# Later modulation rows computed by output columns: a multiply-and-sum along each row on VectorE in place of running sums and a sum over partitions on TensorE

## The chip, the cores and the metric

The kernel runs on one core of one Trainium2 chip. The metric is the device time of one execution in microseconds (us), lower is better. A core has TensorE (PE; its weight loads are listed apart as PEld), VectorE (DVE), ScalarE (ACT), GpSimd (POOL) and SyncE (SP); SP, ACT and POOL also issue DMA transfers.

## The reference, cut to what matters

One layer of a diffusion backbone, batch 1, 1024 tokens of 1024 channels, a context of 256 tokens, everything in float32:

```python
mod_x = jax.nn.silu(c) @ w_ada[l] + b_ada[l]                 # c: (1, 1024), w_ada: (1024, 6 * 1024)
sh1, sc1, g1, sh2, sc2, g2 = jnp.split(mod_x[:, None, :], 6, axis=-1)
h_x = _modulate(_rms_norm(x, norm1_gain[l]), sh1, sc1)       # h * (1 + scale) + shift
y_x, y_c = _token_mixer(h_x, h_c, ...)                       # Fourier branch, retention branch, gates, y @ w_out
x = x + g1 * y_x
h2 = _modulate(_rms_norm(x, norm2_gain[l]), sh2, sc2)
x = x + g2 * _sq_relu_mlp(h2, w_mlp1[l], w_mlp2[l])
return _rms_norm(x, final_gain)
```

Of the six modulation rows of 1024 values, the first two (sh1, sc1) are needed before any projection can start. The change concerns the other four: g1, sh2, sc2 and g2.

## The kernel before, in words

Nearly all the time is TensorE's. Each float32 product of the large projections is made of three products of operands split into a rounded part ("hi") and a remainder ("lo"): `mm3` and its relatives. Weights stream in chunks through a ring: SP loads a chunk into `raw` (256 or 512 KB transfers), ACT writes `ring_hi` (`hi_to`), and POOL subtracts (`lo`, line 1005) to make `ring_lo`. SP loads chunk i only when POOL is done with chunk i-2. All engines run programs written out by hand, each in its own order, joined by semaphores.

The stages in order: modulation rows sh1, sc1 and the input projections (0 to about 350 us); the Fourier and retention output products `four_product`, `ret_product` (to about 435); the gates with Strassen-like products `gate_product` (to about 590); the output projection `out_first`, `out_first_end`, `out_step` with the 16 chunks ("wo", 0) to ("wo", 15) (to about 680); the two MLP products (to the end).

**The output projection**, where most of the rows below lie: it makes 16 groups i of 128 tokens by 512 columns. Groups 0 to 3 are `out_first`; steps 1, 2 and 3 make groups 4 to 7, 8 to 11 and 12 to 15. In steps 1 and 2 the four groups advance together, chunk by chunk, so that all four end shortly one after the other, and group i+4 starts in the PSUM bank that group i has left. It may start when VectorE has done `residual` for that group (two operations, lines 2355 and 2357), which TensorE learns from `o_free`:

```python
if kp == 0:
    pe.wait_ge(o_free, i - 3)
```

**The later modulation rows.** `load_ada(eng, j)` loads, for j = 0 to 31, the 128 x 1024 block of `w_ada` of 128 input channels (j % 8) and of one of the four rows (j // 8), 512 KB each, from 128 rows of the matrix that lie 24 KB apart. `add_row(j)` on VectorE multiplies the block by the 128 values of silu(c) that stand one to a partition, and adds it to a running sum: in `ada_acc` in SBUF for j below 16; for the rest, but the last block of each row, in two banks of PSUM (`ps`). After eight blocks the sum over the 128 partitions is still missing: `reduce_row(a, bank)` on TensorE multiplies `ada_acc` by a column of ones, two halves of 512 columns, in plain float32. It is called four times: after two of the gate products, in step 1 after the last chunk of group 4, and in step 2 before the last chunk. `row_out(a, banks)` on ACT copies the two results out of PSUM (line 1311) and stores them in `mod_scr` in DRAM; g1 and g2 come back from there as broadcast tiles `g1b`, `g2b`, and sh2, sc2 as `mod2`, one value to a partition.

The order that matters on VectorE: in the output projection `residual(0, 0..3)`, then `add_row(18..26)`, then `residual(1, 0..3)`, then `add_row(27..29)`, `z_mean(0, 4)`, the sums on `mod2`, `add_row(30)`, `add_row(31)`. On ACT the loads of blocks 22 to 31 stand between the `hi_to` calls for chunks 7 to 12; each waits until the row that used its buffer before is done. Blocks 18 to 21 are loaded by SP before.

Of the kernel before, what the change touches and what calls it, by code (L numbers as in the profile page):

```python
# [21 lines left out]
P = 128  # L22
D = 1024
# [112 lines left out]
def program(nc, ins, out):  # L136
    with ExitStack() as ctx:
# [141 lines left out]
        hss = small("hss", [P, 3, NT, HEADS])  # L279
        cols = small("cols", [P, 2, 2])  # L280
# [38 lines left out]
        ada_acc = place("ada_acc", o_t + 2048, [P, D])  # L319
        ada_row = place("ada_row", o_t + 6144, [64, 512])  # L320
# [54 lines left out]
        mod_scr = nc.dram_tensor("mod_scr", [4, D], F32, kind="Internal").ap()  # L375
# [71 lines left out]
        ada_acc_done = sem("ada_acc_done")  # L447
        ada_red = sem("ada_red")
        ada_row_out = sem("ada_row_out")
        row_stored = sem("row_stored")  # L450
# [79 lines left out]
        def load_ada(eng, j):  # L530

            if j == 0:
                yr_stored(eng, 1)
            elif j < 18:
                eng.wait_ge(ada_acc_done, j)
            elif j < 21:
                gate_wait(eng, 5, KT - 1)
            else:
                eng.wait_ge(ada_acc_done, {29: 27, 30: 28, 31: 30}.get(j, j - 3))
# [188 lines left out]
        def _(sp):  # L728
# [229 lines left out]
            for s in range(2, STEPS):  # L958
# [5 lines left out]
                if s == 2 * FP + 1:  # L964
                    sp.wait_ge(row_stored, 16 * 8)
                    sp.dma_start(g2b[:], mod_scr[3:4, :].to_broadcast([P, D])).then_inc(gates_in, 16)
# [92 lines left out]
        def _(act):  # L1059
# [166 lines left out]
            for j in range(1, 18):  # L1226
# [77 lines left out]
            def row_out(a, banks):  # L1304

                for half in range(2):
                    act.wait_ge(ada_red, 2 * a + half + 1)
                    if a:
                        act.wait_ge(row_stored, 32 * a)
                    row = ada_row[32 * half:32 * half + 1, :]  # L1310
# [17 lines left out]
            def g_copy(p, m):  # L1328
# [7 lines left out]
                else:  # L1336
# [5 lines left out]
                    else:  # L1342
                        act.wait_ge(ada_acc_done, 4)
# [19 lines left out]
            hi_to(("fo", 2))  # L1363
            load_ada(act, 0)
# [49 lines left out]
            for j in range(1, KT - 3):  # L1414
# [6 lines left out]
                if j == 2:  # L1421
                    row_out(0, 2)
# [12 lines left out]
            row_out(1, 2)  # L1435
# [29 lines left out]
            act.dma_start(g1b[:], mod_scr[0:1, :].to_broadcast([P, D])).then_inc(gate1_in, 16)  # L1465
# [11 lines left out]
            row_out(2, 0)  # L1477
            hi_to(("wo", 10))
            load_ada(act, 29)
            act.wait_ge(row_stored, 16 * 6)  # L1480
            with nc.allow_non_contiguous_dma(reason="2048 modulation values, one per row"):
                for a in range(2):
                    act.dma_start(mod2[:, a, :], mod_scr[1 + a, :].rearrange("(c p) -> p c", p=P)).then_inc(gates_in, 16)
            hi_to(("wo", 11))

            def z_square(t):
                row_added(act, t)
                act.wait_ge(sumsq, 10 + t)
                if t in (0, 4):

                    act.wait_ge(ada_row_out, 6 + t // 2)
# [81 lines left out]
            row_out(3, 0)  # L1573
# [15 lines left out]
            act.wait_ge(row_stored, 16 * 8)  # L1589
# [187 lines left out]
        def _(dve):  # L1777
# [356 lines left out]
            def add_row(jj):  # L2134

                kt = jj % 8
                src = ada_place(jj)
                late = jj >= 16
# [3 lines left out]
                if kt == 7 and late or kt == 0 and 0 < jj < 16:  # L2142

                    dve.wait_ge(ada_red, 2 * (jj // 8))
                if jj == 16:
                    dve.wait_ge(ada_row_out, 4)
                if kt == 0:
                    do.chain(V.tensor_scalar(total, src[:], silu_c[:, 0, 0:1], None, ALU.mult), ada_acc_done)
                else:
                    do.chain(V.scalar_tensor_tensor(ada_acc[:] if kt == 7 else total, src[:], silu_c[:, kt, 0:1], total,  # L2150
                                                    ALU.mult, ALU.add), ada_acc_done)
# [315 lines left out]
            dve.wait_ge(gates_in, 16 * 2)  # L2467
# [20 lines left out]
            dve.wait_ge(row_stored, 16 * 8)  # L2488
# [186 lines left out]
            for s in range(3, STEPS):  # L2675
                down_los(s)
                q, n = s // FP, s % FP
                if s == 2 * FP + 4:
                    dve.wait_ge(gates_in, 16 * 5)
# [41 lines left out]
        def _(pe):  # L2721
# [293 lines left out]
            def reduce_row(a, bank):  # L3015

                pe.wait_ge(ada_acc_done, 8 * (a + 1))
                if a:
                    pe.wait_ge(ada_row_out, 2 * a)
                if a == 2:  # L3020
                    pe.wait_ge(o_free, 4)
                if a == 3:
                    pe.wait_ge(sumsq, 14)
                for half in range(2):
                    M(ps[32 * half:32 * half + 1, bank + half, :], lhsT=ones[:],
# [423 lines left out]
```

## Time and profile before

| | before |
|---|---|
| median of 3 runs | 1307.93 us (1307.86 to 1310.1) |
| profiled execution: from the first to the last instruction (span) | 1306.3 us; its time as a whole is not listed apart, the median lies 1.6 us above the span |
| busy: PE | 1278.7 us (98%) |
| busy: DVE | 875.5 us (67%) |
| busy: ACT | 605.1 us (46%) |
| busy: POOL | 147.0 us (11%) |
| chain that ended last | PE 93%, DVE 3%, DMA 2% |

Busy time is the union of an engine's instructions. A row of the timeline gives the start, the duration, the engine, the line of the kernel, the operation, what it writes and reads by the program's names, and in brackets how long the engine stood idle before it and what ended that. Neighbouring instructions of one kind are merged ("x3"). Matmuls overlap, so that their spacing, not their listed duration, is what one costs.

### The profile page before, as it was taken

To read this page: it belongs to the slowest core of one execution; us is meant where nothing else is said; L and a number is where in the kernel's file an instruction comes from. 1 tells how busy PE (TensorE), PEld (TensorE's weight loads), DVE (VectorE), ACT (ScalarE), POOL (GpSimd) and SP (SyncE) were. 2 spreads that over 40 slices of the span, in tenths; PEclk is the share of its full clock that TensorE was granted. 3 is DMA by queue.
4 is the path that set the end of the run, shared out by engine and by line. 5 is a ranking of instruction groups with operands and counts; after the bars stand their busy time and mean duration, and the time that the engine had idled before them with its cause. 6 is when DMAs were issued, how large, how long until landed. Compare 5 with 4: busy or idle time off the path is not lost.

```text
span 1306.3 us, 16741 instructions
## 1 busy us (share of the span) xinstructions
PE 1278.7 (98%) x6140; PEld 1044.1 (80%) x6140; DVE 875.5 (67%) x1397; ACT 605.1 (46%) x1039; POOL 147.0 (11%) x87
## 2 busy tenths in 40 slices
PE   5999999999999999999999999999999999999997
PEld 1788788888888778888788888888888888888886
DVE  3563577752556987768588766556646568868866
ACT  6871221242123544452668655545555433554444
POOL 0216330102231000014530000000000000000000
PEclk8999999999999999999999999999999999999999
DMA  9414220202256455567852544444438986468634
GB/s 382 154 33 146 81 97 1 65 13 66 65 191 219 146 193 202 182 252 278 297 185 73 191 155 161 137 149 162 151 114 281 316 281 222 162 215 266 192 100 162
DMA packets 95098, 220.09 MB, mean 168 GB/s; under 512 B 12436, under 2 KB 12692, under 8 KB 93992
## 3 DMA queue, kind: packets, MB, share of 16 engines
q1 hardware_dynamic: 83184, 189.58, 42.8%
q10 hardware_dynamic: 10040, 23.15, 4.9%
q0 software_dynamic: 1792, 6.29, 1.4%
q8 instruction: 49, 0.80, 0.3%
q14 instruction: 33, 0.27, 0.1%
HBM read 167.59 MB, written 51.40 MB: 168 GB/s over the span
## 4 chain that ended last, share of the span: by engine, by line
PE 93%; DVE 3%; DMA 2%; issue 1%; ACT 1%; POOL 0%; SPq 0%; ACTq 0%; DVEq 0%
PE ps L2726 16%; PE ps L2728 15%; PE ps L2727 15%; PE ps L3266 8%; PE ps L3274 8%; PE ps L3269 8%; PE ps L3109 4%; PE ps L3104 4%; PE ps L3106 4%; PE ps L3292 3%; PE ps L2804 2%; DMA ada_in<-in_w_ada 2%; PE ps L2930 1%; PE ps L2912 1%; PE ps L2871 1%
## 5 line engine op out<-in xcount | busy, mean ns | idle before, releaser
L1005 POOL TENSOR_TENSOR ring_lo<-raw,ring_hi 128x1024 fp32r<-128x1024 f32 x42 | 102.7, 2458 | 500.4 <-ACT ring_hi L1088 500.3
L2726 PE MATMUL ps<-t_hi,s_hi 128*128 128x512 f32 x392 | 153.1, 391 | 0.0
L2728 PE MATMUL ps<-t_hi,s_lo 128*128 128x512 f32 x392 | 153.1, 391 | 0.0
L2727 PE MATMUL ps<-t_lo,s_hi 128*128 128x512 f32 x392 | 153.1, 390 | 0.0
L1646 ACT ACTIVATE s_hi<-s_raw 128x512 fp32r<-128x512 f32 x112 | 70.5, 630 | 115.2 <-DMA b<-in_w_stream 58.1
L2605 DVE TENSOR_TENSOR s_lo<-s_raw,s_hi 128x512 fp32r<-128x512 f32 x112 | 77.3, 690 | 44.5 <-ACT s_hi L1646 44.0
L2726 PE MATMUL ps<-ring_hi,hT_hi 128*128 128x512 f32 x232 | 94.2, 406 | 0.0
L2728 PE MATMUL ps<-ring_hi,hT_lo 128*128 128x512 f32 x232 | 90.7, 391 | 0.0
L2727 PE MATMUL ps<-ring_lo,hT_hi 128*128 128x512 f32 x232 | 90.5, 390 | 0.0
L2726 PEld LDWEIGHTS ps<-t_hi,s_hi 128*128 128x128 f32 x392 | 73.6, 188 | 16.2 <-DVE t_lo L2609 0.4
L2727 PEld LDWEIGHTS ps<-t_lo,s_hi 128*128 128x128 f32 x392 | 73.6, 188 | 15.9
L2728 PEld LDWEIGHTS ps<-t_hi,s_lo 128*128 128x128 f32 x392 | 73.6, 188 | 15.8
L1088 ACT ACTIVATE ring_hi<-raw 128x1024 fp32r<-128x1024 f32 x46 | 48.2, 1057 | 70.7 <-DMA raw<-in_w_stream 35.3
L1634 ACT ACTIVATE ffa<-ffa 128x512 f32<-128x512 f32 x48 | 30.3, 631 | 71.2 <-DVE ffa L2543 71.2
L2543 DVE TENSOR_TENSOR ffa<-ps,uw 128x512 f32<-128x512 f32 x32 | 22.1, 691 | 44.9 <-PE ps L3274 25.0
L2726 PEld LDWEIGHTS ps<-ring_hi,hT_hi 128*128 128x128 f32 x232 | 43.6, 188 | 10.5 <-issue 1.5
L2728 PEld LDWEIGHTS ps<-ring_hi,hT_lo 128*128 128x128 f32 x232 | 43.5, 188 | 9.6
L3266 PE MATMUL ps<-h_hi,w_T_hi 128*128 128x512 f32 x128 | 50.1, 391 | 0.0
L2727 PEld LDWEIGHTS ps<-ring_lo,hT_hi 128*128 128x128 f32 x232 | 43.7, 188 | 8.0
L3266 PE MATMUL ps<-h_hi,w_B_hi 128*128 128x512 f32 x128 | 50.0, 391 | 0.0
L3269 PE MATMUL ps<-h_lo,w_T_hi 128*128 128x512 f32 x128 | 49.9, 390 | 0.0
L3269 PE MATMUL ps<-h_lo,w_B_hi 128*128 128x512 f32 x128 | 49.8, 389 | 0.0
(474 smaller groups left out, 3151.6 us busy)
## 6 DMA issues: line engine op xcount, KB each, us to landing
s_raw<-ff_scr SPq DMA_DIRECT2D x112, 256.0 KB, 2.9
raw<-in_w_stream SPq DMA_DIRECT2D x34, 512.0 KB, 4.3
ff_scr<-ffs SPq DMA_DIRECT2D x16, 1024.0 KB, 4.8
t_raw<-in_w_stream SPq DMA_DIRECT2D x64, 256.0 KB, 3.5
w_B_raw<-in_w_stream SPq DMA_DIRECT2D x48, 256.0 KB, 2.8
ff_scr<-ffa SPq DMA_DIRECT2D x16, 768.0 KB, 4.5
b<-in_w_stream SPq DMA_DIRECT2D x48, 256.0 KB, 4.3
ada_in<-in_w_ada SPq DMA_DIRECT2D x8, 1024.0 KB, 14.9
```

The costliest lines, as they stand in the source:

```text
L1005: nc.gpsimd.tensor_tensor(lo_ap, raw_of(i), hi_ap.bitcast(F32), ALU.subtract).then_inc(split, 1)
L1646: A(s_slot[n][0][:], s_slot[n][2][:], ACT.Copy).then_inc(down_hi, 1)
L2605: V.tensor_tensor(s_slot[n][1][:], s_slot[n][2][:], s_slot[n][0][:].bitcast(F32), ALU.subtract).then_inc(down_lo, 1)
L2726: M(dst, lhsT=l_hi, rhs=r_hi, start=first, stop=False, skip_group_check=goes_on)
L2727: M(dst, lhsT=l_hi, rhs=r_lo, start=False, stop=False, skip_group_check=goes_on)
L2728: return M(dst, lhsT=l_lo, rhs=r_hi, start=False, stop=last, skip_group_check=goes_on)
L3104: M(ps[:, b, :], lhsT=l_hi[:, w], rhs=m_hi[:, kt, :], start=kt == 0 and not adds, stop=False, skip_group_check=adds)
L3106: M(ps[:, b, :], lhsT=l_hi[:, w], rhs=m_lo[:, kt, :], start=False, stop=False, skip_group_check=adds)
L3109: mm = M(ps[:, b, :], lhsT=l_lo[:, kt * P:(kt + 1) * P], rhs=m_hi[:, kt, :], start=False, stop=kt == 3, skip_group_check=adds)
L3266: M(ps[:, b, :], lhsT=l_hi[:, w], rhs=m_hi[:, kt, :], start=kt == 0 and not adds, stop=False, skip_group_check=adds)
L3269: M(ps[:, b, :], lhsT=l_hi[:, w], rhs=m_lo[:, kt, :], start=False, stop=False, skip_group_check=adds)
L3274: mm = M(ps[:, b, :], lhsT=l_lo[:, w], rhs=m_hi[:, kt, :], start=False, stop=kt == 3 and (p, j) != (6, 0), skip_group_check=adds)
```

## The change

The host splits `w_ada`: the first 2048 columns stay as they are (`w_ada`, now with rows of 8 KB that follow one another), and the last 4096 columns are transposed into `ada_columns`, 32 blocks of 128 output columns by 1024 input channels, each 512 KB in one piece. silu(c) is laid out once along the free dimension: ACT stores `silu_c` to DRAM (`silu_scr`, 1024 values of 4 bytes) and, when the Fourier split is done (`ab_ready`, 7), loads it back as `silu_row`, 128 x 1024, the same row in every partition. `add_row(j)` is then one `tensor_tensor_reduce` on VectorE: block times `silu_row`, summed along the row, 128 finished modulation values, one to a partition. Blocks 8 to 23 write straight into `mod2`; blocks 0 to 7 and 24 to 31 (g1, g2) into `gate_cols`, which ACT stores (`store_gate`) for the broadcast loads. `reduce_row` and `row_out` are gone, with their waits. The loads have the same size, number and order, and the waits for their buffers are the same.

```diff
-        mod_scr = nc.dram_tensor("mod_scr", [4, D], F32, kind="Internal").ap()
+        gate_scr = nc.dram_tensor("gate_scr", [2, D], F32, kind="Internal").ap()
+        silu_scr = nc.dram_tensor("silu_scr", [1, D], F32, kind="Internal").ap()
...
-            eng.dma_start(ada_place(j)[:], ins["w_ada"][(j % 8) * P:(j % 8 + 1) * P, (2 + j // 8) * D:(3 + j // 8) * D]
-                          ).then_inc(ada_landed(j)[0], 16)
+            eng.dma_start(ada_place(j)[:], ins["ada_columns"][j]).then_inc(ada_landed(j)[0], 16)
...
                 if j == 12:
                     act.wait_ge(masked, NT)
+                    with nc.allow_non_contiguous_dma(reason="1024 values of c, one per row"):
+                        act.dma_start(silu_scr[0].rearrange("(c p) -> p c", p=P), silu_c[:, :, 0]).then_inc(silu_stored, 16)
...
-            def row_out(a, banks):
-
-                for half in range(2):
-                    act.wait_ge(ada_red, 2 * a + half + 1)
...
-                    A(row, ps[32 * half:32 * half + 1, banks + half, :], ACT.Copy).then_inc(ada_row_out, 1)
-                    act.wait_ge(ada_row_out, 2 * a + half + 1)
-                    act.dma_start(mod_scr[a:a + 1, half * 512:(half + 1) * 512], row).then_inc(row_stored, 16)
+            def store_gate(a):
+
+                act.wait_ge(mod_done, (8, 32)[a])
+                with nc.allow_non_contiguous_dma(reason="1024 modulation values, one per row"):
+                    act.dma_start(gate_scr[a].rearrange("(c p) -> p c", p=P), gate_cols[:, a, :]).then_inc(gate_stored, 16)
...
+            act.wait_ge(ab_ready, 7)
+            act.wait_ge(silu_stored, 16)
+            act.dma_start(silu_row[:], silu_scr[0:1, :].to_broadcast([P, D])).then_inc(silu_in, 16)
             load_ada(act, 0)
...
-            row_out(1, 2)
...
-            row_out(2, 0)
             hi_to(("wo", 10))
             load_ada(act, 29)
-            act.wait_ge(row_stored, 16 * 6)
-            with nc.allow_non_contiguous_dma(reason="2048 modulation values, one per row"):
-                for a in range(2):
-                    act.dma_start(mod2[:, a, :], mod_scr[1 + a, :].rearrange("(c p) -> p c", p=P)).then_inc(gates_in, 16)
             hi_to(("wo", 11))
...
             def add_row(jj):
 
-                kt = jj % 8
+                a, c = jj // 8, jj % 8
                 src = ada_place(jj)
...
-                total = ps[:, 2:4, :].rearrange("p a b -> p (a b)") if late else ada_acc[:]
+                total = gate_cols[:, a // 3, c:c + 1] if a in (0, 3) else mod2[:, a - 1, c:c + 1]
+                if jj == 0:
+                    dve.wait_ge(silu_in, 16)
                 dve.wait_ge(*ada_landed(jj))
...
-                    do.chain(V.scalar_tensor_tensor(ada_acc[:] if kt == 7 else total, src[:], silu_c[:, kt, 0:1], total,
-                                                    ALU.mult, ALU.add), ada_acc_done)
+                do.chain(V.tensor_tensor_reduce(src[:], src[:], silu_row[:], 1.0, 0.0, ALU.mult, ALU.add, total), mod_done)
...
-            dve.wait_ge(gates_in, 16 * 2)
             do.chain(V.tensor_tensor(mod2[:], mod2[:], bmod2[:], ALU.add))
...
-            def reduce_row(a, bank):
-
-                pe.wait_ge(ada_acc_done, 8 * (a + 1))
...
-                for half in range(2):
-                    M(ps[32 * half:32 * half + 1, bank + half, :], lhsT=ones[:],
-                      rhs=ada_acc[:, half * 512:(half + 1) * 512],
-                      start=True, stop=True).then_inc(ada_red, 1)
...
-                        if (step, kp, t) in ((1, 3, 0), (2, 2, 3)):
-                            reduce_row(step + 1, 0)
...
-        "w_ada": a["w_ada"][0], "b_ada": b_ada,
+        "w_ada": a["w_ada"][0][:, :2 * D], "b_ada": b_ada,
+        "ada_columns": a["w_ada"][0][:, 2 * D:].T.reshape(32, P, D),
```

How it moves instructions, at two places. First VectorE in the output projection, between the last `residual` of groups 0 to 3 and the first of groups 4 to 7. Before (`ada_late_...` and `ada_next` are the four buffers of the loaded blocks, `ps` is PSUM):

```order
L2357 TENSOR_TENSOR acc<-ps,acc 128x512
L2150 SCALAR_TENSOR_TENSOR ps<-ada_late_198,silu_c,ps 128x1024
L2150 SCALAR_TENSOR_TENSOR ps<-ada_late_199,silu_c,ps 128x1024
L2150 SCALAR_TENSOR_TENSOR ps<-ada_late_200,silu_c,ps 128x1024
L2150 SCALAR_TENSOR_TENSOR ps<-ada_next,silu_c,ps 128x1024
L2150 SCALAR_TENSOR_TENSOR ps<-ada_late_198,silu_c,ps 128x1024
L2150 SCALAR_TENSOR_TENSOR ada_acc<-ada_late_199,silu_c,ps 128x1024
L2148 TENSOR_SCALAR ps<-ada_late_200,silu_c 128x1024
L2150 SCALAR_TENSOR_TENSOR ps<-ada_next,silu_c,ps 128x1024
L2150 SCALAR_TENSOR_TENSOR ps<-ada_late_198,silu_c,ps 128x1024
L2355 TENSOR_TENSOR ps<-ps,g1b 128x512
```

The same place in the changed kernel, its last three rows and the first `residual` (`mod_139` is `mod2`; the second instruction of each pair writes the sum out):

```order
L2340 TENSOR_TENSOR acc<-ps,acc 128x512
L2134 ISA ada_late_198,mod_139<-ada_late_198,silu_row 128x1024
L2134 ISA mod_139 128x1
...
L2134 ISA ada_late_200,gate_cols<-ada_late_200,silu_row 128x1024
L2134 ISA gate_cols 128x1
L2134 ISA ada_next,gate_cols<-ada_next,silu_row 128x1024
L2134 ISA gate_cols 128x1
L2134 ISA ada_late_198,gate_cols<-ada_late_198,silu_row 128x1024
L2134 ISA gate_cols 128x1
L2338 TENSOR_TENSOR ps<-ps,g1b 128x512
```

The nine rows keep their place; each is now two instructions, and its second operand of full width lies in SBUF (`silu_row`) and no longer in PSUM.

Second ACT at the same time, from the load of block 26 to the rounding of chunk 11. Before (`ring_hi<-raw` is `hi_to`):

```order
L542 DMA ada_late_198<-in_w_ada 128x1024
L542 DMA ada_late_199<-in_w_ada 128x1024
L542 DMA ada_late_200<-in_w_ada 128x1024
L1311 ACTIVATE ada_row<-ps 1x512
L1313 DMA mod_scr<-ada_row 1x512
L1311 ACTIVATE ada_row<-ps 1x512
L1313 DMA mod_scr<-ada_row 1x512
L1088 ACTIVATE ring_hi<-raw 128x1024
L542 DMA ada_late_198<-in_w_ada 128x1024
L1483 DMA mod_139<-mod_scr 128x8x1 x2
L1088 ACTIVATE ring_hi<-raw 128x1024
```

The same place in the changed kernel:

```order
L543 DMA ada_late_198<-in_ada_columns 128x1024
L543 DMA ada_late_199<-in_ada_columns 128x1024
L543 DMA ada_late_200<-in_ada_columns 128x1024
L1088 ACTIVATE ring_hi<-raw 128x1024
L543 DMA ada_late_198<-in_ada_columns 128x1024
L1088 ACTIVATE ring_hi<-raw 128x1024
```

The copies out of PSUM, their stores and the two loads of `mod2` are gone, and the rounding of chunks 10 and 11 follows the loads directly.

## Rows read from the trace of the kernel before

**Rows 1.** Waits of PE over the span: total us, times, longest us

```profile
PE ps L2830 <- DMA ada_in<-in_w_ada: 15.1, 7, 9.0
...
PE ps L3109 <- DVE g_B_lo L2214: 0.6, 1, 0.6
```

**Rows 2.** Timeline of PE around the third reduce_row: start us, duration us, instruction

```profile
627.61 0.39 PE L2727 MATMUL ps<-ring_lo,yT_hi 128*128 128x512 f32 x1
627.84 0.39 PE L2728 MATMUL ps<-ring_hi,yT_lo 128*128 128x512 f32 x1
628.15 1.03 PE L3025 MATMUL ps<-ada_acc,ones 128*1 128x512 f32 x4
629.11 0.50 PE L2726 MATMUL ps<-ring_hi,yT_hi 128*128 128x512 f32 x1
629.45 0.39 PE L2727 MATMUL ps<-ring_lo,yT_hi 128*128 128x512 f32 x1
```

**Rows 3.** Groups of VectorE by shape, add_row with its sum in PSUM: busy us, mean ns

```profile
L2150 DVE SCALAR_TENSOR_TENSOR ps<-ada_late,silu_c,ps 128x1024 f32<-128x1024 f32 x9 | 11.6, 1290 | 0.4 <-DMA ada_late<-in_w_ada 0.2
```

**Rows 4.** Timeline of VectorE at 307 us, a tensor_tensor_reduce of 512 columns

```profile
307.80 0.69 DVE L2069 CUSTOM_DVE_ANT_0 fj<-u_e,sgn 128x512 f32<-128x512 f32 x1
308.41 0.08 DVE L2069 DVE_READ_ACCUMULATOR2_ANT u_c<- 128x1 f32 x1
```

**Rows 5.** Timeline of VectorE, 594 to 602 us

```profile
594.10 1.23 DVE L2344 TENSOR_TENSOR yT_lo<-yf_in,yT_hi 128x1024 fp32r<-128x1024 f32 x1
595.68 2.99 DVE L2237 TENSOR_TENSOR sig<-sig,yr_in 128x1024 f32<-128x1024 f32 x1 [0.35 <-ACT sig L1358]
598.70 3.30 DVE L2248 TENSOR_TENSOR yf_in<-yf_in,sig 128x1024 f32<-128x1024 f32 x1
```

**Rows 6.** Timeline of POOL at the same time

```profile
595.15 5.77 POOL L1005 TENSOR_TENSOR ring_lo<-raw,ring_hi 128x1024 fp32r<-128x1024 f32 x2 [18.63 <-ACT ring_hi L1088]
```

**Rows 7.** Timeline of POOL, 612 to 635 us

```profile
612.41 4.91 POOL L1005 TENSOR_TENSOR ring_lo<-raw,ring_hi 128x1024 fp32r<-128x1024 f32 x2 [2.27 <-ACT ring_hi L1088]
622.73 4.75 POOL L1005 TENSOR_TENSOR ring_lo<-raw,ring_hi 128x1024 fp32r<-128x1024 f32 x2 [5.40 <-ACT ring_hi L1088]
632.43 2.40 POOL L1005 TENSOR_TENSOR ring_lo<-raw,ring_hi 128x1024 fp32r<-128x1024 f32 x1 [4.95 <-ACT ring_hi L1088]
```

**Rows 8.** Timeline of VectorE, rows 18 to 26 and the residual behind them

```profile
612.44 3.94 DVE L2150 SCALAR_TENSOR_TENSOR ps<-ada_late,silu_c,ps 128x1024 f32<-128x1024 f32 x3
...
621.78 1.28 DVE L2150 SCALAR_TENSOR_TENSOR ada_acc<-ada_late,silu_c,ps 128x1024 f32<-128x1024 f32 x1 [2.62 <-DMA ada_late<-in_w_ada]
625.73 1.29 DVE L2148 TENSOR_SCALAR ps<-ada_late,silu_c 128x1024 f32<-128x1024 f32 x1 [2.67 <-DMA ada_late<-in_w_ada]
...
629.70 0.70 DVE L2355 TENSOR_TENSOR ps<-ps,g1b 128x512 f32<-128x512 f32 x1
```

**Rows 9.** Timeline of PE, the first matmul of group 8

```profile
633.33 0.39 PE L2726 MATMUL ps<-ring_hi,yT_hi 128*128 128x512 f32 x1
```

**Rows 10.** Timeline of ACT, the last z_norm before the transposes

```profile
649.08 1.13 ACT L1506 ACTIVATE xa<-acc,rstd 128x1024 f32<-128x1024 f32 x1
```

**Rows 11.** Timeline of PE, the first transposes that read it

```profile
652.19 1.04 PE L2804 MATMUL ps<-ident,xa 128*128 128x128 f32 x8
```

**Rows 12.** Timeline of VectorE, the operation after add_row(0)

```profile
382.42 0.69 DVE L2164 COPY b_sb<-ps 128x512 f32<-128x512 f32 x1 [0.48 <-PE ps L3060]
```

**Rows 13.** Timeline of ACT, hi_to(("fo", 2)), ahead of the first block's load

```profile
372.90 1.06 ACT L1088 ACTIVATE ring_hi<-raw 128x1024 fp32r<-128x1024 f32 x1 [0.49 <-ACT yr_first L1298]
```

**Rows 14.** Instructions on g1b, a broadcast load of 1024 values: us to landing

```profile
DMA to landing us min/median/max: 6.8/6.8/6.8
```

**Rows 15.** Timeline of POOL at the time of add_row(0)

```profile
378.98 2.41 POOL L1005 TENSOR_TENSOR ring_lo<-raw,ring_hi 128x1024 fp32r<-128x1024 f32 x1 [2.55 <-ACT ring_hi L1088]
```

**Rows 16.** Timeline of PE, four_product(4), which needs VectorE's work behind add_row(0)

```profile
385.74 0.48 PE L2726 MATMUL ps<-ab_hi,ring_hi 128*128 128x512 f32 x1
```

**Rows 17.** Windows of PE in the head: busy, granted clock, DMA share, GB/s

```profile
18.00:28.00 10.00, 6.47 (x28) 0.53 1.01 419
```

More of the change, by code:

```diff
@@ L279, in program @@
         hss = small("hss", [P, 3, NT, HEADS])
+        gate_cols = small("gate_cols", [P, 2, KT])
         cols = small("cols", [P, 2, 2])
@@ L318, in program @@
         b_sb = place("b_sb", o_t, [P, HALF])
-        ada_acc = place("ada_acc", o_t + 2048, [P, D])
-        ada_row = place("ada_row", o_t + 6144, [64, 512])
+        silu_row = place("silu_row", o_t + 2048, [P, D])
         yr_first = [place("yr_first0", o_kv + 12288, [P, SEQ]), place("yr_first1", o_t + 16384, [P, SEQ])]
@@ L446, in program @@
         ada_raw_in = sem("ada_raw_in")
[L447 to L450, printed above, removed]
+        mod_done = sem("mod_done")
+        silu_stored = sem("silu_stored")
+        silu_in = sem("silu_in")
+        gate_stored = sem("gate_stored")
         acc_in = [sem(f"acc_in{i}") for i in range(4)]
@@ L534, in load_ada @@
             elif j < 18:
-                eng.wait_ge(ada_acc_done, j)
+                eng.wait_ge(mod_done, j)
             elif j < 21:
@@ L964, in _ @@
                 if s == 2 * FP + 1:
-                    sp.wait_ge(row_stored, 16 * 8)
-                    sp.dma_start(g2b[:], mod_scr[3:4, :].to_broadcast([P, D])).then_inc(gates_in, 16)
+                    sp.wait_ge(gate_stored, 16 * 2)
+                    sp.dma_start(g2b[:], gate_scr[1:2, :].to_broadcast([P, D])).then_inc(gates_in, 16)
                     sp.dma_start(b2b[:], ins["b_ada"][:, 5 * D:6 * D].to_broadcast([P, D])).then_inc(gates_in, 16)
@@ L1342, in g_copy @@
                     else:
-                        act.wait_ge(ada_acc_done, 4)
+                        act.wait_ge(mod_done, 4)
                 A(dst[:], ps[:, b, :], ACT.Copy).then_inc(up_copied, 1)
@@ L1421, in _ @@
                 if j == 2:
-                    row_out(0, 2)
+                    store_gate(0)
                 g_copy(6, j + 1)
@@ L1464, in _ @@
             act.wait_ge(y_ready, KT - 1)
-            act.dma_start(g1b[:], mod_scr[0:1, :].to_broadcast([P, D])).then_inc(gate1_in, 16)
+            act.wait_ge(gate_stored, 16)
+            act.dma_start(g1b[:], gate_scr[0:1, :].to_broadcast([P, D])).then_inc(gate1_in, 16)
             act.dma_start(b1b[:], ins["b_ada"][:, 2 * D:3 * D].to_broadcast([P, D])).then_inc(gate1_in, 16)
@@ L1572, in _ @@
             z_norm(3)
-            row_out(3, 0)
+            store_gate(1)
             for c in range(4):
@@ L1587, in _ @@
             z_square(6)
-            act.wait_ge(row_stored, 16 * 8)
+            act.wait_ge(mod_done, 32)
             z_modulate_pair(0, (1, 3))
@@ L2134, in add_row @@
             def add_row(jj):
-                kt = jj % 8
+                a, c = jj // 8, jj % 8
                 src = ada_place(jj)
-                late = jj >= 16
-                total = ps[:, 2:4, :].rearrange("p a b -> p (a b)") if late else ada_acc[:]
+                total = gate_cols[:, a // 3, c:c + 1] if a in (0, 3) else mod2[:, a - 1, c:c + 1]
+                if jj == 0:
+                    dve.wait_ge(silu_in, 16)
                 dve.wait_ge(*ada_landed(jj))
[L2142 to L2149, printed above, removed]
-                    do.chain(V.scalar_tensor_tensor(ada_acc[:] if kt == 7 else total, src[:], silu_c[:, kt, 0:1], total,
-                                                    ALU.mult, ALU.add), ada_acc_done)
+                do.chain(V.tensor_tensor_reduce(src[:], src[:], silu_row[:], 1.0, 0.0, ALU.mult, ALU.add, total), mod_done)
             def y_remainder(t):
@@ L2487, in _ @@
             residual(3, 6)
-            dve.wait_ge(row_stored, 16 * 8)
             z_modulate_lower(0)
@@ L2678, in _ @@
                 if s == 2 * FP + 4:
-                    dve.wait_ge(gates_in, 16 * 5)
+                    dve.wait_ge(gates_in, 16 * 3)
                     do.chain(V.tensor_tensor(g2b[:], g2b[:], b2b[:], ALU.add), g_ready)
@@ L3114, in _ @@
                 gate_product(p, m)
-                if (p, m) in ((5, 2), (2, 6)):
-                    reduce_row(m // 6, 2)
             def z_transposes(c):
-                if c == 0:
-                    pe.wait_ge(ada_acc_done, 32)
                 pe.wait_ge(xhat, 10 + 4)
```

13 lines of the change are left out of this document (1 added, 12 removed).

## The prediction

> **What bounds the kernel now.** I read the waits of TensorE first, over the whole span: after the first 45 us, in which it waits 15.1 us for the blocks of `ada_in`, it waits for VectorE once, 0.6 us, at the start of the gates [rows 1]. So the end is set by how many matmuls TensorE has, and an instruction taken off it comes off the time, as long as every other engine delivers that much earlier. Nothing in the page says how much earlier they can; that has to be read from the timelines at each point where the change makes TensorE arrive sooner. The timelines show a second thing: where POOL and VectorE work at the same time, some operations of VectorE take more than twice their time [rows 5, 6].
>
> **What it removes from TensorE.** Around a `reduce_row` the matmuls start 0.23 us apart. The last one before it is followed after 0.31 us in place of 0.23, the four records of the sum take from 628.15 to 629.11, and the first matmul behind is followed after 0.34 in place of 0.23 [rows 2]. That is 0.08 + 0.96 + 0.11 = 1.15 us. There are four calls: 4.6 us, 0.35% of the time.
>
> **One row on VectorE.** Before, 1.29 us and some 0.04 to the next [rows 3]. The new operation stands in the trace at half the width: 0.69 us, its accumulator read starting 0.61 after it and taking 0.08 [rows 4]. A `tensor_tensor` of 1024 columns takes 1.23 [rows 5], 0.54 more than 0.69, so I take 1.23 for the new one, 1.15 to its accumulator read, and 1.26 from row to row. The upper bound would be twice the half-width time and both overheads, 2 x (0.69 + 0.08) = 1.54; the near row decides. By itself this makes VectorE 0.06 us faster per row. The single wait of 0.6 us at the gates has two rows ahead of it on a VectorE without pauses, and shrinks by about 0.1.
>
> **What the row now reads.** In rows 16 to 31 the running sum came from PSUM; the new second operand, `silu_row`, lies in SBUF. At 595.68 an operation with both inputs in SBUF took 2.99 us and the next one 3.30, where a like one just before took 1.23 [rows 5]; POOL's two subtractions then took 5.77 us together [rows 6], against 2.40 for one undisturbed [rows 7]. The times fit strict turns: POOL's first until 597.6, VectorE's until 598.7, POOL's second until 600.9, VectorE's until 602. At 612.44, with POOL at work from 612.41 to 617.32 [rows 7], three rows with their sum in PSUM took 3.94, 1.31 each [rows 8]: no turns. So two inputs in SBUF are what makes an operation take turns with POOL. No row shows the new operation beside POOL; it has two inputs in SBUF, so I take the turns for it. The Trainium skill says the same in "SBUF — State Buffer", section "Who interferes with whom": a VectorE instruction with two SBUF inputs contends with a GpSimd one that reads SBUF. The trace agrees for `tensor_tensor` (2.99 us against 1.23). By that rule the sum below holds; without it the whole 4.6 us would be left.
>
> **Where the turns cost.** Nine rows, 18 to 26, stand between the residuals of groups 0 to 3 and that of group 4. Before, this was harmless: the rows waited 2.62 + 2.67 = 5.3 us for their blocks, and the residual began at 629.70 [rows 8], ended 1.46 later at 631.16, and group 8, which needs that bank, began at 633.33 [rows 9]: 2.2 us to spare. In what follows I stay on the clock of this trace and let the 2.3 us of the first two sums shift everything alike: the loads and residuals here are released by TensorE, or by what it released.
> - Without the third sum (its turn comes between groups 4 and 5 of the same step) TensorE wants the bank at 633.33 - 1.15 = 632.18. With undisturbed rows it is free at 631.16 - 9 x 0.07 = 630.5 at the latest. Nothing is lost.
> - With turns: from 612.44 VectorE has nine rows of 1.26, 11.3 us, and the residual, 1.46. POOL's subtractions for chunks 6, 7, 8 and 9 fall in this time, two from 612.41 and two from 622.73 [rows 7]. Each makes VectorE wait 2.40 less the 0.1 us in which a row only writes its sum out: 4 x 2.3 = 9.2. Sum: 612.44 + 11.3 + 1.46 + 9.2 = 634.4. The blocks are not late in this order, since the pauses for them (5.3 us) are what the turns fill; the loads that ACT holds back until a row is done come some 2 us later, and POOL's input comes no later than before.
> - TensorE then waits 634.4 - 632.18 = 2.2 us at group 8, and 0.1 at each of groups 9 to 11, where a residual (1.46) is slower than a group's part of a chunk (six matmuls, 1.36): 2.5 us. A row that meets no POOL instruction, or a block later than I think, moves this by 0.5 either way.
>
> **The rest of the path, costed at nothing.** The norms before the transposes: the last one ends at 650.21 [rows 10], the transposes start at 652.19 [rows 11]. Without two sums and with the new wait they want it at 652.19 - 2.3 + 2.5 = 652.4; rows 27 to 29 and so the norms come up to 2 us later: they just fit, because ACT loses two copies of PSUM, two stores and two loads there. If that cover is gone, each us late is a us of time. Row 0: it ended 0.48 us before VectorE's next operation could start at 382.42 [rows 12]. Now it also waits for `silu_row`, which ACT issues behind the rounding that ends at 373.96 [rows 13] and which by a like load is 6.8 us on its way [rows 14], so until 381; POOL is at work until 381.4 [rows 15]; with 1.26 us it is done by 382.7. The product that needs what follows starts at 385.74 [rows 16], and three operations like the one at 382.42, 2.1 us, lie between: 0.9 us to spare, or nothing if the load takes 2 us longer. The store of silu(c), the two stores of `gate_cols` and ACT's waits in front of them: hidden, ACT is half idle and the broadcasts come back over 90 us later, or 400. They are 1024 packets of 4 bytes each, as the two loads of `mod2` were. The transposed blocks: same bytes, same number, nothing. The head: in the saturated stretch the blocks of `ada_in`, though 24 KB apart, moved at 419 GB/s [rows 17], all DMA engines busy, so that packing them closer has nothing to give.
>
> **Sum:** -4.6 + 2.5 - 0.1 = -2.2 us in the span of 1306.3, which I put unchanged on the median 1307.93; the 1.6 us around the span stay. I round the gain down to 2.1 for the small things that can only be late: **1305.8 us**.
>
> **Rivals.**
> 1. No turns: the reduce operation reads its operands in a way that leaves POOL alone. For it: no row shows the contrary, and it isn't the operation of [rows 5]. Against it: it has the same two inputs. Then the whole 4.6 us stays: 1307.93 - 4.6 = 1303.3.
> 2. A fifth turn. POOL's chunk 10 began at 632.43 [rows 7], held up by ACT, which copied two rows out of PSUM before rounding it. With that gone it is ready at about 632.0, when row 26 starts at 631.7 to 631.8. If row 26 comes 0.3 us later, POOL is first and the residual slips another 2.3 us. Time: -4.6 + 2.5 + 2.3 = +0.2, 1308.1.
> 3. Slower: the wait becomes long enough to cost the clock. In the head the granted clock stood at 0.53 of full over 10 us, the lower of its two levels for nearly all of it, after TensorE had worked only in pieces [rows 17]; the 0.6 us at the gates cost nothing. With five turns TensorE stands still for 4.8 us at one place. If a pause of that kind drops the clock for 10 us, half of that is lost, 5 us: -4.6 + 4.8 + 5 = +5.2, 1313.1. It decides from a pause somewhere between 0.6 and 4.8 us.
> 4. The new operation runs at half rate: a row then costs 2.3 in place of 1.23 and the nine rows 9 us more: slower by some 7 us. The row of 512 columns with two float32 inputs in SBUF at 0.69 speaks against it [rows 4]. The Trainium skill gives such a rule, "Vector Engine (DVE) Microarchitecture Reference", section 7: one shape of operation with two SBUF sources wider than bf16 is said to halve its throughput. The row disagrees with that for this operation.
>
> That the sums don't leave TensorE at all is no rival: the order of instructions shows all four gone.
>
> **Chances.** Forecast 0.60, rival 1 0.18, rival 2 0.12, rivals 3 and 4 0.10. About 0.2%, 2.6 us, is what a measurement of this kernel can tell from no change. The forecast lies inside it, with a quarter of its chance (0.15) beyond: faster 0.18 + 0.15 = 0.33; within 0.45 + 0.10 = 0.55; slower 0.10 and the bad end of rival 2, 0.02: 0.12. The range reaches from rival 1, with 0.3 us of scatter, to past rival 2, with one of scatter: 1303.0 to 1309.0.
>
> **What would show it.** The row operations at 1.23 us (half rate: 2.3). Beside POOL, between 610 and 632 us, rows of 3.5 us or so in four places (rival 1: all 1.23). A new wait of TensorE of about 2.2 us for VectorE's `acc` at the first matmul of group 8, some 2.3 us earlier than 632.2 on the new clock, and none there in rival 1; 4.5 or more in rivals 2 and 3, and in rival 3 a granted clock under 1 behind it. TensorE busy 4.6 us less in each. It is wrong if TensorE waits at `four_product` or at the transposes, or if the gain exceeds 2.6 us with the turns there.

## The result and the profile after

The changed kernel takes 1315.98 us (median of five, 1314.07 to 1318.01) against 1307.93: a ratio of 1.0061 with a 95% interval of 1.0050 to 1.0072, that is 8.0 us more. The forecast was 1305.8, with a range of 1303.0 to 1309.0: the change is slower by more than the range allowed. The profiled execution took 1315.56, its span is 1313.8 in place of 1306.3.

The waits of TensorE over the whole span (us in total, times, longest us) show three that the kernel before did not have, and a fourth of 0.7 us at the gates:

```profile
PE ps L2785 <- ACT a_raw L1505: 4.8, 1, 4.8
PE ps L2707 <- DVE yf_out L2150: 1.8, 1, 1.8
...
PE ps L2707 <- DVE acc L2340: 1.3, 1, 1.3
...
PE ps L3070 <- DVE sig_b L2212: 0.7, 1, 0.7
```

The 0.6 us of [rows 1], at 438.0 in the gates, is absent. The change need not be why: experiment 6 below is the kernel before up to 482 us and has no such wait either, and experiment 8 has it again. The new wait of 0.7 stands at 490.9. The 1.3 us is group 8 waiting for the residual, which was forecast as 2.2. The first two are at places where the sum had nothing.

I laid the same matmuls of both traces side by side (6124 each, without those of the sums) and read the difference of their starts. It is about 0.5 us up to 385 us (there the profiles of the experiments below lie between -1.1 and +0.3, so these 0.5 say nothing of the change), and then goes like this:

| place (before, us) | step | after it |
|---|---|---|
| 385.7, `four_product(4)` | +2.1 | 2.6 |
| 438.0, the wait of [rows 1] is absent | -0.7 | 1.9 |
| 483.9, first sum gone | -1.1 | 0.8 |
| 489.4, new wait for `sig_b` | +0.7 | 1.5 |
| 555.8 and 629.1, second and third sum gone | -0.9, -1.0 | -0.4 |
| 633.3, group 8 | +1.3 | 1.0 |
| to 637, groups 9 to 11 | +0.3 | 1.3 |
| 650.7, fourth sum gone | -0.9 | 0.3 |
| 657.2, within the transposes | +5.1 | 5.4 |
| to 659.8, TensorE at the lower clock | +2.3 | 7.7 |

Just ahead of the transposes the change stands at +0.3 us; nearly all of the loss falls behind that.

**Group 8.** Timeline of VectorE in the changed kernel, the rows between the residuals, and the residual of group 8's bank:

```profile
613.11 3.21 DVE L2134 CUSTOM_DVE_ANT_0 ada_late<-ada_late,silu_row 128x1024 f32<-128x1024 f32 x1
...
616.37 3.29 DVE L2134 CUSTOM_DVE_ANT_0 ada_late<-ada_late,silu_row 128x1024 f32<-128x1024 f32 x1
...
619.70 1.22 DVE L2134 CUSTOM_DVE_ANT_0 ada_late<-ada_late,silu_row 128x1024 f32<-128x1024 f32 x1
...
622.24 3.30 DVE L2134 CUSTOM_DVE_ANT_0 ada_late<-ada_late,silu_row 128x1024 f32<-128x1024 f32 x1
...
625.58 3.29 DVE L2134 CUSTOM_DVE_ANT_0 ada_late<-ada_late,silu_row 128x1024 f32<-128x1024 f32 x1
...
632.73 0.70 DVE L2338 TENSOR_TENSOR ps<-ps,g1b 128x512 f32<-128x512 f32 x1
```

Four rows take 3.2 to 3.3 us, the other five 1.22 ([rows 3, 8] had 1.29). In POOL's timeline of the same kernel two pairs of subtractions stand beside them, which take 5.73 and 6.52 us, where [rows 7] had 4.91 and 4.75 ("x2" is two merged instructions):

```profile
612.85 5.73 POOL L1005 TENSOR_TENSOR ring_lo<-raw,ring_hi 128x1024 fp32r<-128x1024 f32 x2 [2.36 <-ACT ring_hi L1088]
621.27 6.52 POOL L1005 TENSOR_TENSOR ring_lo<-raw,ring_hi 128x1024 fp32r<-128x1024 f32 x2 [2.70 <-ACT ring_hi L1088]
```

**The transposes.** Timeline of TensorE, then of ACT, at the long wait:

```profile
657.13 0.60 PE L2785 MATMUL ps<-ident,xa 128*128 128x128 f32 x4
662.55 1.09 PE L2785 MATMUL ps<-ident,xa 128*128 128x128 f32 x4 [4.83 <-ACT a_raw L1505]
...
664.72 0.63 PE L2707 MATMUL ps<-ring_hi,yT_hi 128*128 128x512 f32 x1
```

```profile
651.35 1.14 ACT L1498 ACTIVATE xa<-acc,rstd 128x1024 f32<-128x1024 f32 x1
...
654.35 1.14 ACT L1511 ACTIVATE h_hi<-a_raw 128x512 fp32r<-128x512 f32 x2
660.69 1.06 ACT L1088 ACTIVATE ring_hi<-raw 128x1024 fp32r<-128x1024 f32 x1 [5.20 <-DMA raw<-in_w_stream]
661.65 0.76 ACT L1505 ACTIVATE a_raw<-ps,mod,a 128x512 f32<-128x512 f32 x1
```

The norm that answers to [rows 10] ends at 652.5 and the first transposes, which answer to [rows 11], start at 652.54 without a wait: that cover just held. What stops TensorE is the rounding of chunk 15 of `wo` on ACT. It waits 5.2 us for its load, and `z_modulate(5)`, which frees a PSUM bank of the transposes, is queued behind it. Two DMA issues of the changed kernel say why (size, us from issue to landing), the load of chunk 15 at 649.1 and the second gate store at 650.4:

```profile
raw<-in_w_stream SPq DMA_DIRECT2D x1, 512.0 KB, 11.5
...
gate_scr<-gate_cols ACTq DMA_DIRECT2D x1, 4.0 KB, 16.5
```

Before, that load took 6.8 us. The store moves 4 KB in 1024 packets of 4 bytes. Windows of the changed kernel (us, busy times of PE, PEld, DVE, ACT, POOL, then granted clock, DMA share, GB/s):

```profile
648.00:652.00 4.00, 4.00 (x20) 3.30 (x19) 2.15 (x2) 2.27 (x3) 1.54 (x2) 1.00 0.97 397
652.00:656.00 4.00, 4.00 (x27) 3.24 (x26) 1.30 (x2) 2.30 (x4) 1.90 (x1) 1.00 1.16 380
656.00:660.00 4.00, 1.73 (x10) 1.22 (x8) 0.31 (x1) 0.00 (x0) 0.00 (x0) 1.00 0.96 114
660.00:664.00 4.00, 1.45 (x6) 1.38 (x7) 2.17 (x3) 3.08 (x5) 2.18 (x1) 0.59 0.99 236
664.00:668.00 4.00, 4.00 (x16) 3.37 (x15) 2.25 (x5) 1.65 (x4) 3.89 (x4) 0.55 0.84 282
668.00:672.00 4.00, 4.00 (x20) 3.26 (x18) 3.86 (x6) 2.82 (x5) 1.30 (x1) 1.00 0.33 102
```

From 656 to 660 the DMA engines are as busy as before but move 114 GB/s in place of 397. The time is not that of the small packets themselves: by the packet records of this trace the 4-byte ones took 2.0 us in these 4 us, all 16 engines together, and the 4 KB ones 59.6. A 4 KB packet took 0.54 us on average, up to 2.04, where in the kernel before, from 652 to 656, it took 0.16. So with the store in flight the packets of the other transfers became slow. And from 660 to 668 the granted clock is near 0.5, the lower of its two levels, after TensorE had stood still from 657.7; a matmul of 512 columns follows the last after 0.43 us in place of 0.23. That is the 2.3 us at the end of the table.

**The column.** Timelines of VectorE and TensorE at row 0, and the load of its block (issued 376.95):

```profile
384.80 1.22 DVE L2134 CUSTOM_DVE_ANT_0 ada_first<-ada_first,silu_row 128x1024 f32<-128x1024 f32 x1 [3.25 <-DMA ada_first<-in_ada_columns]
```

```profile
388.34 0.47 PE L2707 MATMUL ps<-ab_hi,ring_hi 128*128 128x512 f32 x1 [1.85 <-DVE yf_out L2150]
```

```profile
ada_first<-in_ada_columns ACTq DMA_DIRECT2D x1, 512.0 KB, 7.7
```

Row 0 did not wait for `silu_row`, which had landed at 378.8. It waited for its own block, which was 7.7 us on its way where the same block took 4.0 before. It was also issued 1.4 us later than before (376.95 against 375.56).

### The profile page after: what moved, and what is told of

It reads as the page before. It is cut to its first block, busy times and chain, and to the rows that moved or that the text cites. A ratio compares the mean times of both kernels' runs of the same rounds, so it can differ in the third digit from the quotient of the medians.

```text
span 1313.8 us, 16718 instructions
## 1 busy us (share of the span) xinstructions
PE 1278.4 (97%) x6124; PEld 1045.8 (80%) x6124; DVE 885.3 (67%) x1429; ACT 601.3 (46%) x1031; POOL 150.7 (11%) x87
## 4 chain that ended last, share of the span: by engine, by line
PE 88%; DMA 4%; DVE 3%; issue 2%; ACT 1%; POOL 1%; SPq 0%; ACTq 0%; DVEq 0%
PE ps L2707 15%; PE ps L2709 15%; PE ps L2708 15%; PE ps L3225 8%; PE ps L3233 8%; PE ps L3228 7%; PE ps L3070 3%; PE ps L3075 3%; PE ps L3072 3%; PE ps L3251 3%; PE ps L2785 2%; DMA ada_in<-in_w_ada 1%; PE ps L2911 1%; DMA raw<-in_w_stream 1%; PE ps L2893 1%
## 5 line engine op out<-in xcount | busy, mean ns | idle before, releaser
L1005 POOL TENSOR_TENSOR ring_lo<-raw,ring_hi 128x1024 fp32r<-128x1024 f32 x42 | 106.4, 2547 | 503.3 <-ACT ring_hi L1088 503.1
```

What stands on the lines that cost most here:

```text
L1005: nc.gpsimd.tensor_tensor(lo_ap, raw_of(i), hi_ap.bitcast(F32), ALU.subtract).then_inc(split, 1)
```

## The experiments

The theories after this look: S, the second gate store, by its small packets, delays chunk 15 (some 7 us of the loss); turns with POOL at group 8 (1.3 and what follows); the load of `silu_row` delays row 0's block (1.8). The rivals are named in each expectation. Each kernel was timed beside runs of the kernel before on the same chip, whose median was 1306.98 for the first four and 1307.42 for the last four; so I compare differences to it. The changed kernel's own is +8.0.

**1. The store later.**

```diff
             z_norm(3)
-            store_gate(1)
             for c in range(4):
...
             z_modulate_pair(0, (1, 3))
+            store_gate(1)
```

> Edit: the changed kernel with its second gate store (gate_cols to gate_scr, 1024 packets of 4 bytes) issued some 25 us later, behind the last reader of the stage on ACT's queue. Theory S (the store is what made the load of chunk 15 of wo take 11.5 us instead of 6.8, held ACT's rounding and a_raw behind it, stopped TensorE for 4.8 us and cost it the upper clock for some 7 us, that is about 3.5 more): that load lands within 7 us, TensorE does not wait at the transposes, granted clock 1.00 there, and the time falls by 8 us, from 1316.0 to about 1308. Rival T (the rows and norms come 1 to 2 us late, the loads of the next x start later and crowd the queues by themselves): the load still takes over 9 us, TensorE still waits over 2 us, the time stays above 1312.

Measured: 1309.69, ratio 1.0022 (1.0013 to 1.0031), +2.7 us. Chunk 15 lands after 7.5 us and the wait at the transposes is 0.8 us:

```profile
PE ps L2707 <- DVE yf_out L2150: 2.5, 1, 2.5
...
PE ps L2785 <- ACT a_raw L1505: 0.8, 1, 0.8
```

The clock stays at 1.00 there. Theory S holds and rival T falls, though a wait of 0.8 remains and the time is 1.7 us above the 1308 expected. In the profiled execution the wait at the column was 2.5 us this time, and there the granted clock fell to the lower level between 387 and 394 us; that cost 2.7 us more by the same side-by-side reading, and is part of why only 5.3 of the expected 8 us came back.

**2. The store in 128 packets.** The host puts the gates' blocks in another order, and a partition's eight values lie side by side in the scratch row:

```diff
-                    act.dma_start(gate_scr[a].rearrange("(c p) -> p c", p=P), gate_cols[:, a, :]).then_inc(gate_stored, 16)
+                    act.dma_start(gate_scr[a].rearrange("(p c) -> p c", c=KT), gate_cols[:, a, :]).then_inc(gate_stored, 16)
...
-"ada_columns": a["w_ada"][0][:, 2 * D:].T.reshape(32, P, D),
+"ada_columns": np.concatenate([
+    b.reshape(P, KT, D).transpose(1, 0, 2) if n in (0, 3) else b.reshape(KT, P, D)
+    for n, b in enumerate(a["w_ada"][0][:, 2 * D:].T.reshape(4, D, D))]),
```

> Edit: the changed kernel with the transposed blocks of both gates in another order on the host (row p of block c is output column 8p+c), so that each gate store is 128 packets of 32 bytes instead of 1024 of 4; same bytes, same place in the queues. If the number of packets is what makes the store expensive (theory S, by packets): chunk 15 of wo lands within 7 to 8 us, no wait at the transposes, about 1308 as with the later store. If any store at that place does it (S, by place): as the changed kernel, 1316. Under rival T also 1316 or nearly.

Measured: 1307.30, ratio 1.0000 (0.9991 to 1.0008), +0.3 us: 7.7 of the 8.0 us are back with the store in the same place. Chunk 15 and the store itself, to landing:

```profile
raw<-in_w_stream SPq DMA_DIRECT2D x1, 512.0 KB, 7.5
...
gate_scr<-gate_cols ACTq DMA_DIRECT2D x1, 4.0 KB, 5.2
```

So a store at this place is harmless if it is made of 128 packets of 32 bytes. Number and size of the packets changed together here; which of the two counts is not shown. TensorE still waits 1.6, 1.5 and 0.9 us at the column, at group 8 and at the transposes: with the 0.3 of groups 9 to 11 these nearly pay back the 4.6 us that the change wins by its sums.

**3. `silu_row` loaded earlier.**

```diff
             copy_heads(0)
+            act.wait_ge(ab_ready, 7)
+            act.wait_ge(silu_stored, 16)
+            act.dma_start(silu_row[:], silu_scr[0:1, :].to_broadcast([P, D]))...
             hi_to(("fo", 1))
             copy_heads(1)
             hi_to(("fo", 2))
-            act.wait_ge(ab_ready, 7)
-            act.wait_ge(silu_stored, 16)
-            act.dma_start(silu_row[:], silu_scr[0:1, :].to_broadcast([P, D]))...
             load_ada(act, 0)
```

> Edit: the changed kernel with the broadcast load of silu_row issued 5.5 us earlier on ACT, right behind the first store of yr and ahead of the roundings of chunks fo 1 and fo 2. If the 1.8 us wait of TensorE for yf_out is due to row 0's block, which queues behind silu_row (7.7 us instead of 4.0 to land, and issued 1.4 us later because the store ahead of it landed late): the block lands by 381, row 0 runs before the column that followed it, no wait, 1.8 us gained: 1314.2. If the block is late for itself (its new layout on the host): it still takes over 7 us and the wait of 1.8 us stays: 1316.0.

Measured: 1312.50, ratio 1.0044 (1.0032 to 1.0056), +5.5 us, 2.5 less than the changed kernel, of which the wait explains 1.8. The wait for `yf_out` is gone from the list of waits. The block (first line) and row 0 in VectorE's timeline:

```profile
ada_first<-in_ada_columns ACTq DMA_DIRECT2D x1, 512.0 KB, 4.6
```

```profile
380.93 1.35 DVE L2134 CUSTOM_DVE_ANT_0 ada_first<-ada_first,silu_row 128x1024 f32<-128x1024 f32 x1 [0.18 <-DMA ada_first<-in_ada_columns]
```

The block's layout is the same in both kernels, so it is not that; it is what was in the queues ahead of it. The wait at the transposes is still there (5.3 us), as expected.

**4. The row operand in PSUM.**

```diff
+                row = silu_row[:]
+                if jj >= 16:
+                    row = ps[:, 2:4, :].rearrange("p a b -> p (a b)")
+                if jj == 16:
+                    do.chain(V.tensor_copy(row, silu_row[:]))
-                do.chain(V.tensor_tensor_reduce(src[:], src[:], silu_row[:], ...
+                do.chain(V.tensor_tensor_reduce(src[:], src[:], row, ...
...
             def z_transposes(c):
+                if c == 0:
+                    pe.wait_ge(mod_done, 32)
```

The first transposes wait again for row 31, as before the change, since they write these banks.

> Edit: the changed kernel with silu_row copied once to PSUM (banks 2 and 3, one more copy of VectorE before row 16), and rows 16 to 31 reading their second operand there; the rows' operation is the same, only the place of one operand differs. Theory turns (two inputs in SBUF make a row take turns with POOL): no row over 1.4 us, POOL's subtractions 2.4 us each, VectorE free for group 8 some 9 us earlier, the 1.3 us wait there gone, and POOL's chunks and rows 27 to 31 earlier; time 1.3 us lower if the store stays as bad (1314.7), more if the norms, now 1 to 2 us earlier, also get chunk 15's load out before the store. Rival (the long rows have another cause, such as DMA writes into SBUF at that time): rows of 3.2 us remain, the wait remains, 1316.0.

Measured: 1311.85, ratio 1.0035 (1.0022 to 1.0048), +4.9 us, 3.1 less than the changed kernel. Timelines of VectorE and POOL:

```profile
610.49 1.22 DVE L2139 CUSTOM_DVE_ANT_0 ada_late<-ada_late,ps 128x1024 f32<-128x1024 f32 x1
...
611.75 1.22 DVE L2139 CUSTOM_DVE_ANT_0 ada_late<-ada_late,ps 128x1024 f32<-128x1024 f32 x1
```

```profile
610.14 4.95 POOL L1005 TENSOR_TENSOR ring_lo<-raw,ring_hi 128x1024 fp32r<-128x1024 f32 x2 [2.34 <-ACT ring_hi L1088]
```

All rows from 18 on take 1.22 us, the first four of them beside this pair of POOL's, and the pair takes 4.95 us again. The operation and the blocks are those of the changed kernel; only the place of one operand differs. That settles the turns. The wait at group 8 is gone, and the one at the transposes is 2.8 us; chunk 15 still took 11.1 us to land beside the store. The execution profiled here took 1307.90 us and was the fastest of the six, so the 2.8 us may be less than that wait is in most of them.

**5. The store alone, on the kernel before.**

```diff
             z_norm(3)
...
+                act.dma_start(silu_scr[0].rearrange("(c p) -> p c", p=P), silu_c[:, :, 0]).then_inc(c_in, 16)
             row_out(3, 0)
```

> Edit: the kernel before with one more store on ACT's queue, between z_norm(3) and row_out(3, 0): 1024 values of silu_c, as 1024 packets of 4 bytes, to a scratch row nobody reads; TensorE's sums stay. It is the changed kernel's second gate store without anything else of the change. Theory S: chunk 15 of wo, issued at 647.7, some 2.5 us before the store, lands late (over 9 us instead of 6.8), TensorE waits some 3 to 5 us at the transposes, part of the next 10 us runs at the lower clock: slower by 4 to 8 us. Rival: the store hurts only in the changed kernel, where everything on DMA is 1 to 2 us later: no wait, same as before.

Measured: 1313.96, ratio 1.0041 (1.0026 to 1.0056), +6.5 us by the medians and 5.4 by the ratio; single executions took 1309.4 to 1317.3, and the profiled one is the slowest. In it, chunk 15 and the store to landing, then the wait:

```profile
raw<-in_w_stream SPq DMA_DIRECT2D x1, 512.0 KB, 13.6
silu_scr<-silu_c ACTq DMA_DIRECT2D x1, 4.0 KB, 18.2
```

```profile
PE ps L2807 <- ACT a_raw L1514: 6.7, 1, 6.7
```

One store of 4 KB, with nothing else changed, costs the kernel before 6.5 us, or 5.4 by the ratio: most of what the change lost. The rival falls.

**6. The sums alone away, on the kernel before.**

```diff
-                    M(ps[32 * half:32 * half + 1, bank + half, :], lhsT=ones[:],
-                      rhs=ada_acc[:, half * 512:(half + 1) * 512],
+                    M(ps[32 * half:32 * half + 1, bank + half, 0:2], lhsT=ones[:],
+                      rhs=ada_acc[:, half * 512:half * 512 + 2],
```

The kernel leaves out all but two of the 512 columns of each half of a sum.

> Edit: the kernel before with the eight matmuls of reduce_row over 2 columns in place of 512; the waits, the copies and the rows on VectorE stay (the modulation rows are then wrong in all but a few columns). It measures what the change can give at best. Theory of the prediction: 4.6 us less less some 0.2 to 0.4 for the small matmuls that remain, so 1302.6 to 1303 on a median of 1307. If work behind the sums is on the path too (residuals, norms, chunks), less: 1304 or more, with a new wait in the trace.

Measured: 1305.70, ratio 0.9986 (0.9977 to 0.9994), -1.7 us: the 1302.6 to 1303 of the prediction's theory is missed, and the alternative, 1304 or more with a new wait, came. Timeline of TensorE around the third call, and its waits:

```profile
625.49 0.39 PE L2728 MATMUL ps<-ring_hi,yT_lo 128*128 128x512 f32 x1
625.81 0.20 PE L3025 MATMUL ps<-ada_acc,ones 128*1 128x2 f32 x4
625.94 0.50 PE L2726 MATMUL ps<-ring_hi,yT_hi 128*128 128x512 f32 x1
626.27 0.40 PE L2727 MATMUL ps<-ring_lo,yT_hi 128*128 128x512 f32 x1
```

```profile
PE ps L2804 <- ACT a_raw L1513: 1.0, 1, 1.0
...
PE ps L3104 <- DVE sig_b L2229: 0.7, 1, 0.7
```

A call still costs 0.09 + 0.13 + 0.10 = 0.32 us, so four save 3.3 and not 4.6, and a new wait of 1.0 us stands at the transposes: chunk 15 is only just in time in the kernel before. That can account for the 0.8 and 0.9 us left in experiments 1 and 2 too. The wait of 0.7 us for `sig_b`, at 487.9, is new as well: without the first sum TensorE arrives there earlier. Side by side, the matmuls behind the transposes are 2.5 us earlier, but 0.8 of that stood already at 385 us, where nothing is changed, and 0.9 came by 480, mostly at 438, where the wait of [rows 1] is absent.

**7. The three mends together** (edits 2, 3 and 4).

> Edit: the three mends together on the changed kernel: gate stores of 128 packets of 32 bytes, silu_row loaded 5.5 us earlier, rows 16 to 31 reading it from PSUM. If the three places are all that was wrong, no wait at the gates' column, at group 8 or at the transposes over 0.3 us, granted clock 1.00 behind the head, and 4.6 us less than before: 1302.4 against 1307.0 (faster by 0.35%). If the first store's or silu(c)'s traffic, or the broadcast, costs elsewhere, 1304 or more.

Measured: 1302.89, ratio 0.9959 (0.9948 to 0.9971), -4.5 us: faster than both kernels. All waits of TensorE that are left:

```profile
PE ps L2816 <- DMA ada_in<-in_w_ada: 14.0, 7, 9.1
PE ps L2750 <- issue: 1.8, 1, 1.8
PE ps L2770 <- POOL ring_lo L1005: 0.9, 1, 0.9
PE ps L2824 <- DVE mod_rows L1860: 0.8, 1, 0.8
PE ps L2750 <- ACT ring_hi L1088: 0.6, 1, 0.6
PE ps L3075 <- DVE sig_b L2217: 0.2, 1, 0.2
PE ps L2790 <- ACT xh_b L1498: 0.2, 1, 0.2
```

Only the head's (the first 45 us) and two of 0.2 us remain. Even the wait for chunk 15 is gone: it is issued at 643.6 (645.9 in experiment 6) and lands in 6.7 us beside a store in 128 packets. Side by side the matmuls behind the fourth sum are 4.65 us earlier than in the kernel before.

**8. The same with the stores in 1024 packets, the second one later** (edits 1, 3 and 4).

> Edit: as the version with all three mends, but the second gate store is left at 1024 packets of 4 bytes and issued some 25 us later. The first gate store, near 499 us, stays at 1024 packets of 4 bytes. If the packets' number only matters where the queues are full, the same time as with 128 packets, 1302.4; if the small packets cost anywhere, 1 us or more above it.

Measured: 1303.86, ratio 0.9969 (0.9956 to 0.9981), -3.6 us. It cannot be told from experiment 7, as the intervals overlap. Its profile has waits of 0.7 and 0.8 us at the gates, in place of 0.2, but they stand at 437.3 and 488.4, ahead of the first store, which is issued at 496.9: the store has no part in them. Side by side it falls another 0.6 us behind experiment 7 between 490 and 560 us, in small steps; whether the store, on its way until 508.1, has a part in that stays open.

## Why the prediction was wrong

- **The sums, 4.6 us: right.** Experiment 7 gives 4.5 by the medians (its ratio allows 3.8 to 6.8), and side by side each sum is a step of 1.2. But the kernel before cannot give all of it (experiment 6): chunk 15 has less than 1 us to spare. I had looked at the norms as the cover of the transposes, and not at the rounding that stands among the modulations on ACT's queue.
- **One row at 1.23 us and no half rate: right**, 1.22, and 1.27 from row to row. Missed: the first row of each eight was a `TENSOR_SCALAR`, which took 0.96 us at row 0 and 0.74 at row 8 (1.28 and 1.29 at rows 16 and 24) and costs 1.22 now. The wait of 0.6 us at the gates, which I let shrink by 0.1, comes and goes from one execution to another; without the first sum TensorE waits 0.2 to 0.8 us for `sig_b` near 490. The dearer row 8 is not needed for that: experiment 6 has the 0.7 us with the row still at 0.74.
- **Turns with POOL: right** in mechanism and number, four between 613 and 629. A turn cost 2.0 to 2.1 us where I took 2.3, so TensorE waited 1.3 us and not 2.2; that term was too large by 0.9. Groups 9 to 11 added 0.3 as forecast. Outside the stretch that I looked at, row 31 at 646.70 met POOL too and took 3.44 us. The Trainium skill's rule ("SBUF — State Buffer", "Who interferes with whom") holds for this operation too: 3.3 against 1.22 us with nothing changed but the operand's place. Rival 1 falls.
- **Row 0, "0.9 us to spare": wrong.** I asked when `silu_row` would land, and it landed early. I did not ask what its 512 KB do to the load issued behind it, which took 7.7 us for 4.0: 1.8 us of wait.
- **"The store of silu(c), the two stores of gate_cols ...: hidden": this is the step that failed.** I asked only who waits for the data, and for that the answer was right: nobody does for 90 us or more. I priced the packets by the loads of `mod2`, the same number of 4-byte packets. Those were 2.8 and 5.3 us on their way; the store took 16.5 and held up a load that somebody does wait for. Within the transposes TensorE lost 5.1 us to the wait and 2.3 to the clock; 0.8 to 0.9 us of the wait stay without the store or with the cheap one, so 6.5 us are the store's, where the term was nothing. The times give 5.3 (experiment 1), 7.7 (experiment 2) and 6.5 (experiment 5). No rival had it, which is why even the range was passed.
- **Rival 3** had the right mechanism, a pause that costs the clock, at the wrong place and with too small a chance: its pause comes from the store, not from a fifth turn; ahead of group 8 there was none.

## What to carry to other kernels

A DMA is not free because nobody waits for its data: look at what else is in the queues when it is issued, who waits for that, and whether the new one is many small packets. Lay out the data on the host so that a store writes each partition's values side by side. And when work comes off the bounding engine, look at each point where it waits for another engine for what had under a microsecond to spare. Here the 4.6 us came through only when three such points were mended.

## What was not expected of the hardware

**Stores in small packets are far dearer than loads in small packets.** A store of 1024 values in 4-byte packets took 9.4 to 11.5 us away from the loads at 650 us (near 277, 499 and 680 us, in all kernels that have it) and 16.5 to 18.8 beside them; loads of the same kind took 2.7 to 5.3, and the same values stored in 128 packets of 32 bytes 3.8 to 6.3. Loads and stores already on their way were held up with it: in experiment 5 a store of `x_scr` issued 1.5 us earlier on SP's queue took 12.8 us in place of 7.1.

The packets' own records do not hold that time: nearly all take 9 ns (7 near 277 us), with 4 bytes as with 32. Of the first gate store of the changed kernel, issued at 499.4, all start between 502.06 and 502.76. Then no packet of any transfer starts until 505.77, and the store lands at 510.2. The window between has a DMA share and a rate of 0:

```profile
503.00:505.00 2.00, 2.00 (x10) 1.65 (x10) 1.97 (x4) 1.50 (x3) 0.00 (x0) 1.00 0.00 0
```

The Trainium skill ("DMA: Bandwidth & Descriptors", "Why small descriptors are slow (HBM only)") puts the fixed cost of a packet at about three cycles of an internal bus. No run here counts such cycles, and a cost within the 9 ns would not explain these stores: spread evenly, 1024 packets are 64 for each of 16 DMA engines, an estimate of 0.6 us where the landing takes 9.4 or more. What in the chip takes the rest no run here shows.

**Pauses and the clock.** Pauses of TensorE of 1.3, 1.6 and 1.85 us in these traces left the granted clock at 1.00. In pauses of 2.5 us (experiment 1, at the column), 2.8 (experiment 4), 4.8, 5.3 and 6.7 it fell to the lower level, and stayed there for 3.4 us (experiments 3 and 4) or 6.8 in all, the rest of the pause included. So a late load can cost more than its wait: 2.3 us on top of 4.8 in the changed kernel, 2.7 on top of 2.5 in experiment 1.
